# Adaptive norms applied behind their projections, and their modulation summed on VectorE

## The reference

```python
def second_block(x, c, norm_g, ada_w, ada_b, ...):
    cond = jax.nn.silu(c)                       # (1, 1024)
    for l in range(2):
        mod = cond @ ada_w[l] + ada_b[l]        # (1, 3072)
        shift, scale, gate = jnp.split(mod, 3, axis=-1)
        h = rms_norm_2(x, norm_g[l]) * (1.0 + scale[:, None, :]) + shift[:, None, :]
        y = even_mixer(h, ...) if l == 0 else odd_mixer(h, ...)
        x = x + gate[:, None, :] * y
```

## Time and profile before

| | |
|---|---|
| median of three runs | 1429.78 us |
| the profiled execution | 1430.1 us, span 1428.3 us |
| mean granted TensorE clock | 0.978 of 2.4 GHz |
| busy: TensorE, its weight loads | 95%, 91% of the span |
| busy: VectorE, ScalarE, GpSimd | 64%, 57%, 6% |
| traffic | 239.98 MB, 168 GB/s on average |

### The profile page before, as it was taken

One profiled execution on the slowest core, in us unless ns is written; L12 is line 12 of the kernel. 1 busy time (PEld: TensorE's weight loads), 2 busy tenths in 40 slices (PEclk: granted clock), 3 DMA queues, 4 the chain that ended last, 5 costly groups with the idle time before them and its releaser, 6 DMA issues.

```text
span 1428.3 us, 27604 instructions
## 1 busy us (share of the span) xinstructions
...
## 2 busy tenths in 40 slices
...
GB/s 193 246 231 244 208 196 104 196 175 116 224 232 247 218 139 126 240 229 250 186 104 120 102 104 45 118 172 236 229 265 173 75 164 130 116 143 150 124 120 30
DMA packets 63314, 239.98 MB, mean 168 GB/s; under 512 B 7025, under 2 KB 8449, under 8 KB 63105
## 3 DMA queue, kind: packets, MB, share of 16 engines
...
HBM read 237.76 MB, written 1.05 MB: 167 GB/s over the span
## 4 chain that ended last, share of the span: by engine, by line
PE 74%; DVE 12%; ACT 9%; issue 4%; DMA 2%; DVEq 0%; ACTq 0%; SPq 0%
PE bank L1735 19%; PE bank L1737 19%; PE bank L1736 19%; DVE w_lo L1045 5%; ACT w_hi L580 3%; PE bank L1742 2%; ACT ada_raw L656 2%; PE bank L1807 2%; PE bank L1808 1%; PE bank L1800 1%; PE bank L1743 1%; PE bank L2101 1%; DMA raw<-w 1%; ACT arena L989 1%; PE bank L1972 1%
## 5 line engine op out<-in xcount | busy, mean ns | idle before, releaser
L1045 DVE TENSOR_TENSOR w_lo<-raw,w_hi 128x1024 fp32r<-128x1024 f32 (+1 forms) x376 | 493.4, 1316 | 344.5 <-ACT w_hi L580 344.3
L1735 PE MATMUL bank<-x_hl,w_hi 128*128 128x272 f32 (+1 forms) x1776 | 517.1, 291 | 16.9 <-DVE w_lo L1045 16.7
L1737 PE MATMUL bank<-x_hl,w_lo 128*128 128x272 f32 (+1 forms) x1776 | 511.4, 288 | 0.0
L1736 PE MATMUL bank<-x_hl,w_hi 128*128 128x272 f32 (+1 forms) x1776 | 509.7, 287 | 0.0
L580 ACT ACTIVATE w_hi<-raw 128x1024 fp32r<-128x1024 f32 (+1 forms) x376 | 413.8, 1106 | 130.4 <-PE bank L1737 108.4
L1735 PEld LDWEIGHTS bank<-x_hl,w_hi 128*128 128x128 f32 x1776 | 336.5, 189 | 19.5 <-DVE w_lo L1045 9.8
L1736 PEld LDWEIGHTS bank<-x_hl,w_hi 128*128 128x128 f32 x1776 | 339.0, 191 | 0.6
L1737 PEld LDWEIGHTS bank<-x_hl,w_lo 128*128 128x128 f32 x1776 | 335.8, 189 | 0.0
L1735 PE MATMUL bank<-a_hi,w_hi 128*128 128x272 f32 (+1 forms) x960 | 280.5, 292 | 14.6 <-DVE a_lo L1157 3.5
L1737 PE MATMUL bank<-a_hi,w_lo 128*128 128x272 f32 (+1 forms) x960 | 276.7, 288 | 0.0
L1736 PE MATMUL bank<-a_lo,w_hi 128*128 128x272 f32 (+1 forms) x960 | 276.4, 288 | 0.0
...
## 6 DMA issues: line engine op xcount, KB each, us to landing
...
```

The costliest lines, as they stand in the source:

```text
L1045: ve.tensor_tensor(w_lo[:, s, 0:n], raw[:, s, 0:n], w_hi[:, s, 0:n].bitcast(F32), ALU.subtract).then_inc(w_lo_ready, 1)
L1735: te.matmul(dst, w_hi[:, s, a:a + P], rhs_hi, start=first, stop=False)
L1736: te.matmul(dst, w_hi[:, s, a:a + P], rhs_lo, start=False, stop=False)
L1737: return te.matmul(dst, w_lo[:, s, a:a + P], rhs_hi, start=False, stop=last)
```

## The change

**Modulation.** The host lays `ada_w` out with output channels on partitions and gives the conditioning vector on every partition (`c_rows`, 512 KB, loaded in gu0). ScalarE takes its silu once, in gu0. One VectorE instruction multiplies a block by it and accumulates along the free axis into one column of `mod` (L1138 of the changed kernel). ScalarE's copies, the three adds and TensorE's sums go. At the start of a gu stage it stands behind the four gate operations rather than ahead of them. The table of bands is loaded in ein rather than in cin.

**Both adaptive norms.** `enter` and `first_quad` now serve ein too: the products start on h * gs, and units are 258 columns wide, since two columns behind the tokens hold the shift vector; their products are the shift's projection, which the last column of the bank yields. r has a 1 there. Each eviction takes two steps: VectorE multiplies the bank by r into one of two buffers (`hg_scaled`, L1435; `scaled_unit`, L1592), then ScalarE adds the last column as a bias and applies the function (`hg_evict`, L875; `shifted`, L975), then come w_hi and w_lo of the unit four further on. In ein TensorE's sum for r stands ahead of unit 3.

**ein.** The value units are computed like the others (v = 16 to 19) and transposed by TensorE; pooled input comes last with tokens on partitions, scaled by r per partition. The levels stand behind units 9, 10, 11, 13, 14, 16 and 17.

**eout to oin.** The residual's add, h * gain, its halves and its square follow each output unit of eout. oin's first three units run behind it with three products of 258 columns per chunk (`fox_first`), then the sum of squares; all of oin uses three products instead of two.

```diff

-
-                sc.wait_ge(ada_in, 16 * i + 16)
-                for c in range(DC):
-                    last = sc.activation(ada_raw[:, c, :], ada_raw[:, c, :], ACT.Copy, scale=cond[:, c:c + 1])
-                last.then_inc(act.step(phase, "am"), 1)
...
+            def shift(l):
+
+                sc.activation(x_hl[:, :, 0, SEQ:SHIFTED], mod[:, l, 0, :].unsqueeze(2).broadcast_to([P, DC, 2]), ACT.Copy).then_inc(act.step(f"sh{l}", "hi"), 1)
 
...
             def hg_evict(v):
-                hg_done(v)
-                func = ACT.Sigmoid if v < 4 else ACT.Copy if v < 8 else ACT.Silu
-                sc.activation(hg[HG_PLACE[v]], bank[HG_BANK[v]][:, 0:SEQ], func).then_inc(act.step("hg", f"e{v}"), 1)
+
+                sc.wait_ge(vec.sem, vec.at("hg", f"m{v}"))
+                func = ACT.Sigmoid if v < 4 else ACT.Silu if 8 <= v < 16 else ACT.Identity
+                sc.activation(hg[HG_PLACE[v]], silu_t[:, v % 2, 0:SEQ], func, bias=silu_t[:, v % 2, SEQ:SEQ + 1]
+                              ).then_inc(act.step("hg", f"e{v}"), 1)
 
...
+            def shifted(u):
+
+                sc.wait_ge(vec.sem, vec.at(f"d{u}", "d"))
+                sc.activation(fox_unit(u), silu_t[:, u % 2, 0:SEQ], ACT.Identity, bias=silu_t[:, u % 2, SEQ:SEQ + 1]
+                              ).then_inc(act.step(f"c{u}", "c"), 1)
 
             def fox_square(name, j, u, e):
-                sc.wait_ge(vec.sem, vec.at(f"d{u}", "d"))
+                sc.wait_ge(act.sem, act.at(f"c{u}", "c"))
                 sc.activation(sq[:, e, 0:SEQ], fox_unit(u), ACT.Square).then_inc(act.step(f"{name}{j}", "sq"), 1)
...
+                def ada(phase, i):
+
+                    flat = ada_raw[:, :, :].rearrange("p a b -> p (a b)")
+                    ve.wait_ge(ada_in, 16 * (12 * k + i) + 16)
+                    ve.scalar_tensor_tensor(flat, flat, 1.0, cond, ALU.mult, ALU.mult,
+                                            accum_out=mod_flat[:, bass.ds(12 * k + i, 1)]).then_inc(vec.step(phase, "ar"), 1)
...
                 gate(g + "q", 0, bank[4])
                 up(g + "q", 0, bank[6])
                 gate(g + "q", 1, bank[7])
                 up(g + "q", 1, bank[3])
+                if k == 0:
+                    ve.wait_ge(act.sem, act.at("cond", "c"))
+                ada(g + "q", 0)
...
+            def hg_scaled(v):
+                ve.wait_ge(unit_done, SLOTS * FIRST_QUAD["ein"] + v + 1)
+                if v >= 2:
+                    ve.wait_ge(act.sem, act.at("hg", f"e{v - 2}"))
+                ve.tensor_tensor(silu_t[:, v % 2, 0:SHIFTED], bank[HG_BANK[v]][:, 0:SHIFTED], r_one, ALU.mult
+                                 ).then_inc(vec.step("hg", f"m{v}"), 1)
+
+            ve.wait_ge(act.sem, act.at("prees", "r"))
...
+            for v in range(9, HG_UNITS):
+                hg_scaled(v)
+                hg_split(v + 4)
+                if v in HG_LEVEL:
+                    tot = hg_level(HG_LEVEL[v], tot)
+                    hg_scores(HG_LEVEL[v])
 
...
+            def eout_add(c):
+
+                ve.wait_ge(unit_done, SLOTS * FIRST_QUAD["eout"] + c + 1)
+                ve.scalar_tensor_tensor(h[:, c, META:T], out1_bank("eout", c // SLOTS, c % SLOTS)[:, 0:SEQ], mod[:, 0, 2, c:c + 1],
+                                        h[:, c, META:T], ALU.mult, ALU.add).then_inc(vec.step("preo", f"h{c}"), 1)
+
+            def eout_lower(c):
+                ve.wait_ge(act.sem, act.at("preo", f"hi{c}"))
+                ve.scalar_tensor_tensor(x_lo[:, c, 0:SEQ], h[:, c, META:T], gain("preo", c), x_hi[:, c, 0:SEQ].bitcast(F32),
+                                        ALU.mult, ALU.subtract).then_inc(vec.step("preo", f"lo{c}"), 1)
+
...
+            def scaled_unit(u):
+
+                ve.wait_ge(unit_done, SLOTS * FIRST_QUAD["oin"] + u + 1)
+                if u >= 2:
+                    ve.wait_ge(act.sem, act.at(f"c{u - 2}", "c"))
+                ve.tensor_tensor(silu_t[:, u % 2, 0:SHIFTED], fox_bank(u)[:, 0:SHIFTED], r_one, ALU.mult).then_inc(vec.step(f"d{u}", "d"), 1)
...
+            def token_sum(phase, dst, n):
+                te.wait_ge(pool.sem, pool.at(phase, "tr2"))
+                te.matmul(dst[:, 0:n], ones[:, :], sq8[:, 0, 0:n], start=True, stop=True).then_inc(pe.step(phase, "ss"), 1)
+
...
+            for v in range(9, 18):
+                hg_unit(v)
+                if v in HG_LEVEL:
+                    hg_level(HG_LEVEL[v])
```

524 lines of the change are left out of this document (259 added, 265 removed).

## The result

The change makes the kernel slower, and by more than I forecast: 1469.03 us, median of four runs (1467.38 to 1472.6), against 1429.74 us of the kernel before beside it. The ratio is 1.0275, 95% interval 1.026 to 1.029. The direction was right, the size was not: +39.3 us where I had +22.8, and outside my range. The profiled execution has a span of 1466.2 us, 37.9 above that of before.

What follows compares the result with a forecast made beforehand. The prediction took the kernel to be bound by matmuls on average (TensorE 95% busy). Its terms summed as 1430.1 + 6.2 + 3.4 + 5 - 7.3 + 1 + 14.5 = 1452.9, by the median 1452.6 us, range 1429 to 1466.

Steps and rivals of the forecast that it cites:

- Entrance into ein, -2: Start of ein: applying the norm factor behind the products gains 9.5 us, of which only 2 remain when unit 4 starts.
- Levels, +4.6: Level loop of ein: VectorE needs 43.2 us against TensorE's 38.6 and becomes the bound, 4.6 us slower.
- The tail of ein, -1: End of ein: the new order can take away about 1 us of its 3 us of stalls.
- eout to oin, -7.3: Passage from eout to oin: oin starts at once instead of after 8.1 us, 7.3 us gained (5 to 8).
- Gates of oin, +1: Eight gate units of oin: VectorE's 2.96 us per unit against 2.87, 1 us lost with the wider products.
- Clock, +3.4 in gu0 and gu2: Gate/up stages gu0 and gu2: longer idle stretches before quad 2 bring half clock, 3.4 us lost (0 to 5).
- Modulation, +6.2: Gate/up stages: the VectorE operation behind the gates delays quad 2's weight loads, 6.2 us lost (4 to 8).
- Pairs, +14.5: Pairs of oin: scaling behind softmax and norms delays the maxima 2.2 us in each of six periods, 14.5 in all.
- Rival 1: Late evictions in pairs and levels stay hidden, only the entrances count, maxima stay 13.45 us apart: 1424 us, chance 0.15.
- rival 3: VectorE's multiply with accumulation takes a second pass, 1.1 us more at each of four entrances: 1459 us, chance 0.1.
- rivals 2 and 5: In the pairs, half the period's delay shows: 1437 us, chance 0.14; or clock falls, 1.5 us per period: 1465, 0.06.
- rival 4: Gains and losses cancel, the entrances being worth what the pairs cost: 1430 us, chance 0.05.

## Why the prediction was wrong

**Entrance into ein, -2:** right. Unit 4 came 2.5 us earlier relative to res3's sum (1146.1 - 1120.08 before, 1141.8 - 1118.29 after), behind GpSimd's tree as forecast. The tree itself took 5.35 us, not the 7.09 of the earlier trace rows, and ended at 1135.5, not 1137 to 1139. The chain of units behind it was a step of its own (+3): there 3.70 us of waiting and 1.7 of half clock were measured.

**Levels, +4.6:** the mechanism was right (VectorE idle for w_hi, TensorE waiting for the products), and undoing it, with the query product's place, gave 3.9 us.

**The tail of ein, -1:** wrong in sign. It cost 5.1 us by the runs; by the trace 3.95 idle and 2.5 at half clock behind it. I counted the stalls of before that the new order removes and did not walk through what it waits for: three units side by side need three weights, and the third stood behind ScalarE's token copies.

**eout to oin, -7.3:** right as far as the gap goes (its working gives 8.1 - 0.25 = 7.85; the 0.55 less has no source in it). The first product of oin starts 0.38 us behind the last of eout (1266.39, 1266.77). It was not worth its size, though, because the factor came later than the three units it allowed, and started the backlog.

**Gates of oin, +1:** this is the step that failed most. The stretch from oin's first product to the first maxima cost 15.6 us where I had 1.6, and the run that undoes the order of the gates gave 13.0 us, by the traces 9.5 us in this stretch. What is left of it above my forecast, some 4.5 us, no run isolates. I wrote "the same 2.96 against 2.87" and took the difference of the rates. That is right for a chain that starts level. But it starts three units behind, and a chain that is slower than TensorE never works them off; a kernel in which the chain gives 1.47 us a unit (before, and again with the skewed loop) does. Measured were 3.09 against 2.95. I had the three numbers, 2.96, 2.87 and the three finished units, and did not put them together.

**Clock, +3.4 in gu0 and gu2:** right for gu0 (first matmul 0.59 us long), not for gu2, where 2.58 us of idle time left the clock at 1.00. The 3.4 us at half clock that I took had 3.1 us in the earlier trace rows as the nearest row; gu0 then showed 3.4. But I priced the clock only there. Of the kernel after, windows behind four of the new waits:

```profile
42.60:46.00 3.40, 3.36 (x15) 3.36 (x16) 3.37 (x7) 1.67 (x3) 0.00 (x0) 0.50 0.57 160
569.30:572.70 3.40, 3.40 (x29) 3.35 (x28) 3.37 (x8) 1.84 (x4) 0.00 (x0) 1.00 0.61 190
1237.50:1242.50 5.00, 5.00 (x23) 5.00 (x24) 0.52 (x2) 0.00 (x0) 0.00 (x0) 0.50 0.38 108
1160.60:1164.00 3.40, 3.33 (x15) 3.36 (x16) 1.90 (x3) 2.78 (x5) 0.00 (x0) 0.51 0.56 155
```

The stretches at 1160, 1237 and 1292 lose 1.7, 2.5 and 2.4 us (half of 3.4, half of 5.0, 0.47 of 5.0), 6.6 in all, none of it in my sum.

**Modulation, +6.2:** wrong in sign with the clock term beside it, which makes +9.6 against 2.9 gained in the run that has this part alone. gu0's term held. In gu2 and gu3 the later issue was there, but shorter loads took it up (0.1 and 0.3 us arrived at TensorE), and what the removed copies would give at the end of gu3, 3 us of TensorE's time, I did not look for. Another 4.5 us of this stretch is luck: the unchanged code near 300 us and in the attention heads ran 1.5 and 3.0 us shorter in the changed kernel's trace, by the clock. I read the places where the new operation stands, not those where the old ones stood.

**Pairs, +14.5:** right in mechanism, place and size of the period, 15.72 us where I had 15.7. The swap that undoes it gave 12.5. The sum over the pairs was right in part by luck: the first distance grew by 2.3 us (12.65 to 14.97) where I had 3.0, and the last by 1.6 (9.35 to 10.94), which I did not have.

Rival 1 (the chains have slack) falls with the maxima, rival 3 with the 1.22 us, rivals 2 and 5 with the period of 15.72, which is neither half the delay nor longer by half clock; rival 4 with the time.
